# Fewer PSUM banks for the fill tiles, one bank for the rope sums, and a moved order of VectorE and ScalarE in the mixer of a 1-core decoder

## The reference

```python
proj = h @ w_in
na_q, na_k, na_v, g_q, g_k, g_v = jnp.split(proj, IN_SPLIT_POINTS, axis=-1)
na_out = neighbourhood_attention(na_q, na_k, na_v, rpb, rows)         # 8 heads of 64
g_q = apply_axial_rope(rms_norm(g_q, q_norm), cos, sin)               # 8 heads
g_k = apply_axial_rope(rms_norm(g_k, k_norm), cos, sin)               # 2 heads
gqa_out = gqa_block_attention(g_q, g_k, g_v)
x = x + jnp.concatenate([na_out, gqa_out], axis=-1) @ w_out
# then: x += memory cross attention (keys from mem @ w_mem_kv), x += conv_ffn
```

## Time and profile before

| | |
|---|---|
| median of 3 runs | 2026.52 us (2026.03 to 2026.71) |
| the profiled execution | 2026.03 us, of which the span is 2024.2 us |
| TensorE busy | 1964.3 us (97%) |
| VectorE busy | 1326.1 us (66%) |
| ScalarE busy | 1094.6 us (54%) |
| GpSimd busy | 210.1 us (10%) |
| chain that ended last | PE 82%, DVE 7%, ACT 5%, issue 2%, POOL 1% |

### The profile page before, as it was taken

The page is one execution under the profiler, slowest core; times in us unless marked ns, Lnnn a source line. Parts: engine busy times, 40 slices in busy tenths (PEclk is TensorE's granted clock), DMA queues, the critical chain, the costliest instruction groups (busy, mean ns, idle before and its releaser), DMA issues.

```text
span 2024.2 us, 30515 instructions
## 1 busy us (share of the span) xinstructions
PE 1964.3 (97%) x12072; PEld 1720.0 (85%) x12072; DVE 1326.1 (66%) x2316; ACT 1094.6 (54%) x1862; POOL 210.1 (10%) x240
## 2 busy tenths in 40 slices
PE   6999999999999999999998999999999999999999
PEld 6878998887899978889986788888888997778887
DVE  5767976576697665555676875555555576786554
ACT  5666765465676554445556454444444565545442
POOL 1231121033112100000024000000000012200000
PEclk9999999999999999999999999999999999999999
DMA  6434556543455646555442255555555453235553
GB/s 256 136 119 128 191 185 232 174 132 112 135 181 182 202 158 199 186 182 173 150 147 95 84 168 192 181 184 185 189 181 188 148 165 126 86 105 188 187 182 128
DMA packets 90110, 329.92 MB, mean 163 GB/s; under 512 B 9968, under 2 KB 10352, under 8 KB 89584
## 3 DMA queue, kind: packets, MB, share of 16 engines
q1 hardware_dynamic: 89968, 327.97, 49.3%
HBM read 326.88 MB, written 1.05 MB: 162 GB/s over the span
## 4 chain that ended last, share of the span: by engine, by line
PE 82%; DVE 7%; ACT 5%; issue 2%; POOL 1%; ACTq 0%; DVEq 0%
PE PS L83 79%; PE PS L86 3%; ACT WH L92 2%; DVE WL L98 2%; DVE TMP L108 1%; ACT TMP L95 1%; DVE SM L114 1%; ACT TMP L94 1%; DVE TMP L98 1%; ACT TMP L92 1%; DVE TMP L105 0%; DVE SM L108 0%; DVE SM L98 0%; POOL SQ L111 0%; POOL M L104 0%
## 5 line engine op out<-in xcount | busy, mean ns | idle before, releaser
L98 DVE TENSOR_TENSOR WL<-RAW,WH 128x1024 fp32r<-128x1024 f32 x608 | 745.8, 1232 | 533.2 <-ACT WH L92 526.6
L92 ACT ACTIVATE WH<-RAW 128x1024 fp32r<-128x1024 f32 x608 | 640.8, 1058 | 542.4 <-PE PS L83 537.2
L83 PE MATMUL PS<-WH,GH 128*128 128x512 f32 (+1 forms) x912 | 361.4, 396 | 3.6 <-DVE WL L98 2.4
L83 PE MATMUL PS<-WL,GH 128*128 128x512 f32 (+1 forms) x912 | 353.8, 388 | 0.0
L83 PE MATMUL PS<-WH,GL 128*128 128x512 f32 (+1 forms) x912 | 353.6, 388 | 0.0
L83 PE MATMUL PS<-GH,WH 128*128 128x256 f32 x1104 | 316.4, 287 | 1.0 <-issue 0.4
L83 PE MATMUL PS<-GH,WL 128*128 128x256 f32 x1104 | 312.6, 283 | 0.0
L83 PE MATMUL PS<-GL,WH 128*128 128x256 f32 x1104 | 312.6, 283 | 0.0
L83 PE MATMUL PS<-WH,HH 128*128 128x512 f32 (+1 forms) x736 | 279.0, 379 | 0.0
L83 PE MATMUL PS<-WH,HL 128*128 128x512 f32 (+1 forms) x736 | 276.5, 376 | 0.0
L83 PE MATMUL PS<-WL,HH 128*128 128x512 f32 (+1 forms) x736 | 276.4, 376 | 0.0
(11 more groups left out here) (143 smaller groups left out, 2388.4 us busy)
## 6 DMA issues: line engine op xcount, KB each, us to landing
RAW<-wts SPq DMA_DIRECT2D x608, 512.0 KB, 4.1
M<-bias SPq DMA_DIRECT2D x2, 2048.0 KB, 13.5
X<-x SPq DMA_DIRECT2D x2, 512.0 KB, 6.1
TMP<-mem SPq DMA_DIRECT2D x1, 1024.0 KB, 12.4
out<-X SPq DMA_DIRECT2D x4, 256.0 KB, 3.4
CST<-cst SPq DMA_DIRECT2D x1, 706.0 KB, 10.4
M<-gf SPq DMA_DIRECT2D x1, 512.0 KB, 5.1
PAR<-par SPq DMA_DIRECT2D x1, 368.0 KB, 7.5
```

The costliest lines, as they stand in the source:

```text
L83: return Issued(self.eng and self.eng.matmul(o, l, r, start=first, stop=last, skip_group_check=share))
L92: return Issued(self.eng.activation(o, i, f, scale=scale))
L98: return Issued(self.eng and self.eng.tensor_tensor(o, a, b, op))
```

## The change

Five edits, in all engines' programs for the mixer of the first block:

1. The sums of squares go to bank 7 alone, all five tiles side by side in it, and VectorE reads all of them at once in `rope_scales` (2 instructions of 10 columns) in place of 2 of 2 columns in each of five `rope(m)`.
2. The fills no longer use bank 7: 3 banks in place of 4.
3. ScalarE takes its steps by `NA_RATES`, and its `others()` has one yield less for each rope tile.
4. VectorE splits the next weight half before `rope_all(m - 2)` in place of behind it.
5. The keys' scales are turned over before the product mk 2 in place of behind it; VectorE copies mk 2 later.

```diff
-        NA_PARTS = [3, 3, 3] + [1, 1, 1] + [1, 2, 1] * 2 + [1, 1, 1]
...
                 def rope(m):
                     e.wait_ge(squared, ("rope", L, m))
-                    ps = take(("sw", L, m), WT + STB)
+                    if m == 0:
+                        take(("rs", L), STB)
                     for t in range(2):
-                        o = S + 2 * t
-                        i = e.mm(ps[:, o:o + 2], SQ[:, m % 3, t * 128:t * 128 + 128], cc(C_BL, 2), True, True)
+                        o = t * 10 + 2 * m
+                        i = e.mm(PS[7][:, o:o + 2], SQ[:, m % 3, t * 128:t * 128 + 128], cc(C_BL, 2), True, True)
                     i.then_inc(summed, ("rope", L, m))
+                    ps = take(("sw", L, m), WT)
                     e.wait_ge(aout, ("rope", L, m))
...
                     for m in range(5):
-                        fm_tile(("rope", L, m), mix, WT + STB)
+                        fm_tile(("rope", L, m), mix, WT)
...
                 fill.rest()
+                e.wait_ge(wide, ("gk", L))
+                put_over(("gk", L), [SQ[:, 3, t * 128:t * 128 + 128] for t in range(2)], WT)
                 fm_tile(("mk", L, 2), mkv, WT)
-                e.wait_ge(wide, ("gk", L))
-                put_over(("gk", L), [SQ[:, 3, t * 128:t * 128 + 128] for t in range(2)], (BANK["gvt", L],))
...
                         rope(m)
-                        if m % 2 == 0:
-                            yield
                         if m < 4:
                             memory(2 * m)
                             memory(2 * m + 1)
-                        if m % 2 == 1:
-                            yield
...
-                run(attention(("na", L), na_heads(L), [256, 256], fill, NA_PARTS))
+                run(attention(("na", L), na_heads(L), [256, 256], fill, NA_RATES))
...
                     e.wait_ge(spread, key)
-                    if m == 0:
-                        e.wait_ge(small)
-                    for t in range(2):
-                        o = 10 * t + 2 * m
-                        e.ts(smc(o, 2), bank(key)[:, S + 2 * t:S + 2 * t + 2], RX2[:, t:t + 1], EPS, ALU.mult,
-                             ALU.add).then_inc(small)
...
                 def rope_scales():
+                    e.wait_ge(summed, ("rope", L, 4))
+                    e.wait_ge(small)
+                    v3 = smc(0, 20).rearrange("p (t n) -> p t n", t=2)
+                    for t in range(2):
+                        m = e.ts(v3[:, t, :], PS[7][:, t * 10:t * 10 + 10], RX2[:, t:t + 1], EPS, ALU.mult, ALU.add)
+                    m.then_inc(dout, ("rs", L))
+                    e.wait_ge(dout)
...
                     for m in range(5):
+                        lows(("rope", L, m))
                         if m >= 2:
                             rope_all(m - 2)
-                        lows(("rope", L, m))
...
+                lows(("mk", L, 2))
                 memory_key(1)
-                memory_key(2)
-                lows(("mk", L, 2))
 
                 def onward():
                     lows(("mk", L, 3))
+                    memory_key(2)
                     yield
```

More of the change, by code:

```diff
@@ L644, in others @@
                 def others():
-                    yield from tm_wide(("v", L), mix, 512, WT + STB)
+                    yield from tm_wide(("v", L), mix, 512, WT)
                     for m in range(2, 4):
-                        fm_tile(("nk", L, m), mix, WT + STB)
+                        fm_tile(("nk", L, m), mix, WT)
                         yield
                     for m in range(5):
-                        fm_tile(("rope", L, m), mix, WT + STB)
+                        fm_tile(("rope", L, m), mix, WT)
                         if m >= 1:
@@ L653, in others @@
                         yield
-                    fm_tile(("gv", L), mix, WT + STB)
+                    fm_tile(("gv", L), mix, WT)
                     rope(4)
                     yield
-                    fm_tile(("mk", L, 0), mkv, WT + STB)
-                    ps = take(("gvt", L), WT + STB)
+                    fm_tile(("mk", L, 0), mkv, WT)
+                    ps = take(("gvt", L), WT)
                     e.wait_ge(ready, ("gv", L))
@@ L663, in others @@
                     yield
-                    fm_tile(("mk", L, 1), mkv, WT + STB)
+                    fm_tile(("mk", L, 1), mkv, WT)
                     yield
```

## The result

| | before | changed |
|---|---|---|
| median | 2026.62 us (2026.03 to 2027.05, 4 runs) | 2045.06 us (2043.83 to 2047.0, 4 runs) |
| ratio of the runs | | 1.0088, 95% interval 1.0076 to 1.0101 |
| profiled execution / span | 2026.03 / 2024.2 us | 2045.22 / 2043.4 us |
| mean granted clock of TensorE | 0.997 | 0.994 |

The changed kernel is slower, by 18.4 us or 0.9%. I had forecast 2039.1 with a range to 2042. The direction and the places were right, the size was too small by 6.

What follows compares the result with a forecast made beforehand. TensorE, busy 97%, bounds the neighbourhood attention; the VectorE, ScalarE and GpSimd chain paces the grouped attention. Waits, the later chain start (6.19 us) and a copy (0.33) give 6.52 us a layer, twice 13.0: 2039.1 us, range 2034 to 2042.

Steps and rivals of the forecast that it cites:

- Part 1: Sums of rope tiles 0 and 2: TensorE waits for ScalarE's later squares, 1.40 and 1.38 us, together 2.78 us a layer.
- Part 2: Before rope tile 4, with three banks: TensorE waits 2.43 us for VectorE to read swap 1 behind a weight half.
- Rival A: Rope tile 4: VectorE's reading of swap 1 does not hold it up; 4.9 us less, 2034.2 us; chance 0.11.
- Part 4: Key scales ahead of mk 2: TensorE waits 2.14 us for GpSimd's copies; grouped-attention chain 6.19 us later, 6.52 with the copy.
- Part 3: Sums read at once in `rope_scales`: the scales come 0.1 us later; the other four pairs' removal is worth 0.
- The sum of the waits: All parts through the start of the grouped-attention chain and mk 2's later copy: 6.52 us a layer, 13.0 us in all.
- nothing was given back: Behind the grouped-attention scores: no lost time returns, as TensorE is busy again or the chain starts from the same scores.
- The check on the clock: TensorE behind the added 1.4 to 2.4 us waits: no clock fall seen; if one, 2.2 us per 24 instructions.
- rival C: Waits of over 2 us, two a layer: TensorE's clock falls, 8.8 us more, 2047.9 us; chance 0.05.

Runs made afterwards that it cites:

- b_act: The kernel before with only ScalarE's new step order (`NA_RATES`, fewer yields) added: 2031.67 us, ratio 1.0024.
- a_dve: The changed kernel with VectorE's rope work put back ahead of the weight half: 2035.78 us, ratio to before 1.0055.
- a_gk: The changed kernel with mk 2 put back ahead of the turning over of the key scales: 2045.67 us, ratio to before 1.0101.
- a_keep: The changed kernel with 14 unread products added in the waits before rope tile 4 and before the scales' turning over, each layer: 2038.83 us, ratio to before 1.0065.
- b_banks: The kernel before with only the bank edits added (sums of squares in bank 7, three banks for the fills): 2032.74 us, ratio 1.0027.
- a_act_dve: The changed kernel with ScalarE's step order and VectorE's weight-half order both taken back: 2029.70 us, ratio 1.0021.
- b_early: The kernel before with rope scales ahead of mk 0's weight half, key scales turned over ahead of mk 2, mk 2 copied later: 2024.51 us, ratio 0.9995.
- b_gk: The kernel before with only the key scales turned over ahead of mk 2 and mk 2 copied later: 2029.01 us, ratio 1.0014.
- b_dve: The kernel before with only VectorE's next weight half moved ahead of the rope work: 2028.95 us, ratio 1.0011.
- a_act: The changed kernel with ScalarE's steps put back as before: 2043.35 us, ratio to before 1.0089.

## Why the prediction missed: right steps, one term at zero

**Part 1, the late squares: right.** Measured from the start of the tile before, with the tile lengths of before, TensorE was due at the sums of tile 0 at 67.50 + (69.14 - 66.19) = 70.45 (66.19 is where tile 0 began before) and began at 71.74: 1.29 us, forecast 1.40. For tile 2 it is 83.73 - (79.49 + 2.97) = 1.27, forecast 1.38. The profile's "idle" is shorter (1.12, 1.11) because the modelled end of the last product overlaps the wait. b_act shows this part alone.

**Part 2, the bank behind the weight half: right.** Due at 83.73 + 1.23 = 84.96, begun at 87.42: 2.46 us, forecast 2.43. Rival A is out: the wait is there in both layers of the profiled execution (2.11 and 2.12 us idle). a_dve takes it out. What I had not said is how edits 3 and 4 shield each other: without edit 3 the same wait is 3.39.

**Part 4, the scales: right.** mk 1 began at 102.77, and the last tile of this kind took 2.97: 107.86 - (102.77 + 2.97) = 2.12 us, forecast 2.14. That the same wait would have come from the bank of mk 0 with the old order, a_gk shows; I had priced edit 5 as if it alone made this wait.

**Part 3, the sums at once: not told apart.** No run isolates it; the forecast of the wait for the scales contains its 0.1 us and fits.

**The sum of the waits: right.** For a whole layer, from the scores of heads 4 and 5 to the last weighing of the grouped attention, the profiles give these starts, of before (first and second layer) and then of after:

```profile
131.19 1.08 PE L83 MATMUL PS<-TMP,M 128*64 128x256 f32 x8 [0.78 <-ACT TMP L92]
...
490.44 1.08 PE L83 MATMUL PS<-TMP,M 128*64 128x256 f32 x8 [0.78 <-ACT TMP L92]
```

```profile
142.20 1.08 PE L83 MATMUL PS<-TMP,M 128*64 128x256 f32 x8 [0.78 <-ACT TMP L92]
...
511.19 1.08 PE L83 MATMUL PS<-TMP,M 128*64 128x256 f32 x8 [0.78 <-ACT TMP L92]
```

The first layer lost (142.20 - 131.19) - (66.03 - 64.71) = 9.69 us. Rope tile 4 was 4.48 - 2.96 = 1.52 slower for the clock. The turning over and mk 2 took 112.85 - 107.86 = 4.99, where the same two, with the clock up, took 3.49 in a_keep: 1.50. What is left is 9.69 - 3.02 = 6.67, forecast 6.52. The last row of each layer still waits 0.78 us for ScalarE, in both kernels: the chain behind the scores was only moved, and nothing was given back, as forecast.

**The check on the clock: this is the step that failed.** It said that waits of 1.4 to 2.4 us lie between 0.60, where the clock was seen to stay, and 8.89, where it was seen to be down, and then I took the price 0, "the rows so far show no such fall". Rows that show neither case are no evidence for zero. The true term is 3.0 us a layer, 6.0 in all; I had priced it in rival C, at 2.2 for each of four waits, 8.8, with a chance of 0.05. The mechanism of rival C came, on top of the waits that I had summed, with 1.5 for each wait: it does not slow the whole tile, since behind the turning over the products of mk 2 are 0.21 us apart up to 111.54 and 0.12 apart from 111.69 on.

The zero was wrong for a second reason, which I overlooked: the trace of the kernel before does show such falls, further on in the program, at 755, 1154 and 1792 us. Here is the first, with its wait and the granted clock behind it, and then the same place in the changed kernel:

```profile
754.62 0.75 PE L83 MATMUL PS<-WH,GH 128*128 128x512 f32 x1 [2.40 <-DVE WL L98]
...
755.00:760.00 5.00, 5.00 (x17) 3.89 (x17) 2.97 (x3) 0.68 (x1) 0.00 (x0) 0.69 0.69 222
```

```profile
775.12 0.50 PE L83 MATMUL PS<-WH,GH 128*128 128x512 f32 x1 [2.16 <-DVE WL L98]
...
775.00:780.00 5.00, 4.88 (x21) 4.05 (x22) 4.14 (x5) 1.33 (x2) 0.00 (x0) 1.00 0.66 198
```

The kernel before has a fall behind 2.40 us idle, and these rows could be read before the prediction. The row that I did use, 8.89 us at the start, shows a clock that is low, but not one that fell: only 8 products had run by then. (The granted clock of that stretch reads 1.00 all the same, so at the start the distance of the products is the better witness.)

The Trainium skill (TensorE: Matmul & The Clock Gate, "A second HAM failure mode: psum-queue depth-cycling") had said that short idle times between groups, in a kernel that cycles through banks, can be enough. The trace of the changed kernel agrees as far as short idle times go, with 0.76 to 0.79 granted in the four stretches behind waits of 1.95 to 2.12 us. But the page speaks of frequent small idle times, and here one single wait of 2 us in otherwise dense work was followed by a fall.

A clean account of the 19.2 us between the two profiled executions: 2 x 9.7 in the two layers, 1.3 at the start, and the rest of the program 1.5 us shorter. The 1.3 at the start has nothing to do with the change: in the same instructions of both kernels the granted clock is 0.83 from 35 to 45 us in the profile of the changed kernel, and 1.00 in that of before. It was 0.83 in the profiles of b_banks, a_gk, a_keep, a_act_dve and b_early too, and 1.00 in those of b_act, b_gk, b_dve, a_act and a_dve. The 1.5 is the fall at 755 us that only the kernel before had: from 754.62 to its next wait of 0.3 us or more, at 861.25, it takes 106.63 us, and the changed kernel from 775.12 to 880.14 takes 105.02. So one fall more and one fall less, outside the change, happen to cancel.

## What to carry to other kernels

When a change moves an instruction, follow the queues of all engines that hand over in that stretch for the next few microseconds: here a square moved on ScalarE, a weight half moved on VectorE and a bank taken away on TensorE were worth 5.4, 2.6 and 6.4 us each. In company the prices shift: taken back under the others, edit 3 gives 2.9 us of waits (5.5 alone) and edit 4 gives 4.7 (2.8 alone). So prices of single edits are measured in the company in which they are kept, by taking them back as well as by adding them, and what the clock did is counted apart from the waits before they are added up. And a wait of about 2 us put into a dense TensorE can have a second price, the slow products behind it. Look for that in the granted clock of the whole program, not only of the stretch that changes; where it goes both ways, the price belongs in the range.

## What the runs showed of the hardware

How long TensorE was idle, and what its clock did behind it, in the two layers of the change: behind 0.60 us and behind 1.12 us (b_act, b_dve, a_dve and others) it did not fall. Behind 1.82 and 1.83 us (b_gk) and 1.89 us (b_banks, a_gk) it stayed at 1.00 in the first layer and fell in the second. Behind the wait for the scales of 1.95 to 1.98 us it fell in both layers of the changed kernel, of a_dve and of a_act, and stayed at 1.00 in both of a_act_dve. Behind 2.11 and 2.12 us (the changed kernel, a_gk) and 3.38 and 3.39 us (a_act, 0.81 granted from 84 to 93 us) it fell each time.

The rest of the program, in the same twelve profiles, shows that the length of one wait does not decide. At the wait that the kernel before has at 754.62, 2.40 us idle in four kernels, the clock fell in the kernel before and in b_dve and stayed up in b_act and b_gk. Behind the waits of 2.18 to 2.22 us that the kernel before has at 1073.71 and 1712.15, and each of the others too, it fell in 3 of 24 (both of b_act, one of a_gk). And it fell where no wait was over 0.60 us: 0.51 granted from 1154 to 1157 us of the kernel before, behind 0.56 us idle and sixteen products of one column. What decides is left open: no run moves a wait without changing something else.

One fall cost 1.5 us as a rule (1.6 at 754.62, 2.6 behind the 3.38 us of a_act). Filling about 1.7 of the 2.0 to 2.1 us idle with products whose result is thrown away kept the clock up in both layers and made a program with more work 6 us faster.
